# Streaming only the changed columns in the doubling inverse of a chunked delta-rule recurrence

## The reference

```python
def step(S, inp):
    r_t, w_t, k_t, v_t, kk_t, a_t = inp
    sa = jnp.einsum('bhvk,bhk->bhv', S, -kk_t)
    S = (S * w_t[:, :, None, :] + sa[..., None] * (kk_t * a_t)[:, :, None, :]
         + v_t[..., None] * k_t[:, :, None, :])
    return S, jnp.einsum('bhvk,bhk->bhv', S, r_t)
```

## Time and profile before

| What | Value |
|---|---|
| Time, median of 3 runs | 2047.01 us (2044.65 to 2049.49) |
| The profiled execution, its own time | 2045.39 us |
| Its span in the trace | 2043.6 us |
| TensorE busy | 1925.4 us, 94% |
| VectorE busy | 1462.8 us, 72% |
| ScalarE busy | 766.4 us, 38% |
| The recurrence stage in the trace | about 405 to 613 us |

### The profile page before, as it was taken

How to read it: one execution, slowest core, us unless ns; L and a number is a source line. 1 busy time by engine, 2 the same in 40 slices (tenths; PEclk the granted TensorE clock), 3 DMA queues, 4 the chain that set the end, 5 groups by cost and what they waited for, 6 DMA issues and landing times. The chain is left out here.

```text
span 2043.6 us, 35100 instructions
## 1 busy us (share of the span) xinstructions
PE 1925.4 (94%) x13881; PEld 1658.6 (81%) x13881; DVE 1462.8 (72%) x3152; ACT 766.4 (38%) x1177; POOL 333.4 (16%) x317
## 2 busy tenths in 40 slices
PE   6999998888989969999999999899779999999999
PEld 6998666677774469999999999799668888888887
DVE  4243343555545056999999999999968888888887
ACT  5332335222214133343334433477623333333332
POOL 1001100000000000333133222000322222322220
PEclk9999999999999979999999999899989999999999
DMA  3222111000003054886688668257979999999996
GB/s 132 86 92 83 32 32 62 25 30 3 3 3 165 0 187 128 327 309 243 240 320 320 251 240 306 66 173 215 299 266 366 334 341 338 341 345 339 339 336 253
DMA packets 175395, 407.24 MB, mean 199 GB/s; under 512 B 16768, under 2 KB 99968, under 8 KB 174208
## 3 DMA queue, kind: packets, MB, share of 16 engines
q1 hardware_dynamic: 132320, 255.96, 36.7%
q0 software_dynamic: 39744, 144.72, 18.8%
q10 hardware_dynamic: 3168, 4.33, 0.6%
HBM read 358.77 MB, written 46.14 MB: 198 GB/s over the span
## 5 line engine op out<-in xcount | busy, mean ns | idle before, releaser
L89 PE MATMUL eo_ps<-vh,e_wh 128*128 128x512 f32 x768 | 300.6, 391 | 12.6 <-DVE e_wl L1958 12.6
L90 PE MATMUL eo_ps<-vh,e_wl 128*128 128x512 f32 x768 | 300.2, 391 | 0.0
L91 PE MATMUL eo_ps<-vl,e_wh 128*128 128x512 f32 x768 | 300.2, 391 | 0.0
L1565 POOL DMA_INDIRECT g_stage<-in_u_rows,gidx x112 | 137.1, 1224 | 837.2 <-DVE gidx L1661 683.2
L1907 ACT CAST vh<-vraw 128x1024 fp32r<-128x1024 f32 x128 | 134.2, 1049 | 323.1 <-PE eo_ps L91 312.7
L1949 DVE TENSOR_TENSOR vl<-vraw,vh 128x1024 fp32r<-128x1024 f32 x128 | 156.7, 1224 | 73.2 <-ACT vh L1907 73.0
L1924 POOL DMA_INDIRECT e_rows<-in_v,gidx x128 | 137.2, 1072 | 391.2 <-DVE e_acc_t L1938 353.7
L89 PE MATMUL h_ps<-x2h,h_uh 128*128 128x384 f32 x520 | 180.9, 348 | 2.7 <-DVE h_ul L1418 2.7
L89 PEld LDWEIGHTS eo_ps<-vh,e_wh 128*128 128x128 f32 x768 | 145.1, 189 | 43.9 <-DVE vl L1949 10.0
L91 PE MATMUL h_ps<-x2l,h_uh 128*128 128x384 f32 x520 | 174.8, 336 | 0.0
L90 PE MATMUL h_ps<-x2h,h_ul 128*128 128x384 f32 x520 | 174.7, 336 | 0.0
(11 more groups left out here) (307 smaller groups left out, 4202.7 us busy)
## 6 DMA issues: line engine op xcount, KB each, us to landing
vraw<-in_v SPq DMA_DIRECT2D x128, 512.0 KB, 6.5
g_stage<-in_u SPq DMA_DIRECT2D x63, 512.0 KB, 6.6
e_hid<-HID_scratch SPq DMA_DIRECT2D x128, 192.0 KB, 6.9
h_uraw<-in_u SPq DMA_DIRECT2D x45, 512.0 KB, 5.2
wraw<-in_w_z SPq DMA_DIRECT2D x43, 512.0 KB, 3.5
HID_scratch<-h_hid SPq DMA_DIRECT2D x106, 192.0 KB, 4.1
G_scratch<-g_stage SPq DMA_DIRECT2D x16, 1024.0 KB, 11.8
gm<-G_scratch SPq DMA_DIRECT2D x128, 128.0 KB, 5.3
```

What stands on the lines that cost most here:

```text
L89: nc.tensor.matmul(out, a[0], b[0], start=start, stop=False)
L90: nc.tensor.matmul(out, a[1], b[0], start=False, stop=False)
L91: return nc.tensor.matmul(out, a[0], b[1], start=False, stop=stop)
L1565: nc.gpsimd.indirect_dma_start(urows[:, j % GBUF_R], None, d["u_rows"], bass.IndirectOffsetOnAxis(ap=gidx[:, j:j + 1], axis=0)).then_inc(r ...
```

## The change

Joining two blocks of size m changes only part of the columns: with kind 0 the first block's columns of each pair, with kind 1 the second's. The kernel before streams and adds all 48 columns, most of the results being zero. The changed kernel streams, writes, masks and adds only the columns of half `h` of each block pair. For levels 0, 1 and 2 (m = 2, 4, 8) these are 24 columns in runs of m. For levels 3 and 4 (m = 16, 32) the last pair is incomplete, and the columns are one run: 16 at level 3; at level 4 it is 32 for line 1079 and the mask, and 16 for line 1089 and the addition. In PSUM the results lie densely; in SBUF the moving operand of the matmuls and the operands of VectorE are read and written in these runs. The weights of every product stay 48 columns wide. Since `off` is also used as weights, the columns that aren't written must be zero, so `off` becomes one buffer per level and is cleared once at the start of the stage.

The widths of kind 0 and kind 1 differ at level 4 and their columns differ everywhere, so the one addition per group at line 998 becomes one per kind: four a level instead of two (at level 4 still two). Line 1079 of the next level waits only for the addition of kind 0 of its group.

```diff
-        off = sb("off", [P, NP4, C])
+        off = sb("off", [P, NLEV, NP4, C])
...
+        def width(lv, h):
+            m = LEVELS[lv]
+            return C // 2 if C % (2 * m) == 0 else min(m, C - h * m)
+
+        def blocks(x, lv, h):
+            m = LEVELS[lv]
+            if C % (2 * m) == 0:
+                return (x.rearrange("r (j h m) -> r j h m", h=2, m=m)[:, :, h] if len(x.shape) == 2 else
+                        x.rearrange("r q (j h m) -> r q j h m", h=2, m=m)[:, :, :, h])
+            c = slice(h * m, h * m + width(lv, h))
+            return x[:, c] if len(x.shape) == 2 else x[:, :, c]
...
+            nc.vector.memset(off[:], 0.0).then_inc(started, 1)
...
-                    nc.vector.tensor_tensor(off[0:R, g * HP:g * HP + HP],
-                                            ps[0:R, OFF[g], 0:HP * C].rearrange("p (a b) -> p a b", a=HP),
-                                            mlev[0:R, lv:lv + 1].broadcast_to([R, HP, C]), ALU.mult).then_inc(off_out, 1)
+                    nc.vector.tensor_tensor(
+                        blocks(off[0:R, lv, q], lv, 0),
+                        dense(ps[0:R, OFF[g], 0:HP * w].rearrange("p (a b) -> p a b", a=HP), lv, 0),
+                        blocks(mlev[0:R, lv:lv + 1].broadcast_to([R, HP, C]), lv, 0), ALU.mult).then_inc(off_out, 1)
...
-                    x0 = kinds(lv)[0]
-                    i = inv[0:R, b, x0:2, g * HP:g * HP + HP]
-                    nc.vector.tensor_tensor(i, i, ps[0:R, 4 + g, x0 * HP * C:2 * HP * C].rearrange(
-                        "p (x a b) -> p x a b", x=2 - x0, a=HP), ALU.add).then_inc(grown_out, 1)
+                    for x in kinds(lv):
+                        w = width(lv, x)
+                        i = blocks(inv[0:R, b, x, g * HP:g * HP + HP], lv, x)
+                        o = ps[0:R, 4 + g, x * HP * w:(x + 1) * HP * w].rearrange("p (a b) -> p a b", a=HP)
+                        nc.vector.tensor_tensor(i, i, dense(o, lv, x), ALU.add).then_inc(grown_out, 1)
...
-                        pe.wait_ge(grown_out, n * 2 + g - 1)
+                        pe.wait_ge(grown_out, grown_outs(c, lv - 1, g) + 1)
...
-                        mm = nc.tensor.matmul(ps[t, OFF[g], p % HP * C:p % HP * C + C], mb[t, b, p, 0:C],
-                                              inv[t, b, 0, p], start=True, stop=True)
+                        mm = nc.tensor.matmul(dense(ps[t, OFF[g], p % HP * w:p % HP * w + w], lv, 0), mb[t, b, p, 0:C],
+                                              blocks(inv[t, b, 0, p], lv, 0), start=True, stop=True)
...
-                            a, m = (inv[t, b, 1, p], off[t, p]) if x == 0 else (off[t, p], inv[t, b, 1, p])
-                            mm = nc.tensor.matmul(o, a, m, start=True, stop=True)
+                            a, m = (inv[t, b, 1, p], off[t, lv, p]) if x == 0 else (off[t, lv, p], inv[t, b, 1, p])
+                            mm = nc.tensor.matmul(o, a, blocks(m, lv, x), start=True, stop=True)
```

More of the change, by code:

```diff
@@ L889, in order, with dense, grown_outs @@
                 recur(NCH - 1, (NCH - 1) % 2, lv)
+        def width(lv, h):
[8 more added lines that the diff above has]
+            return x[:, c] if len(x.shape) == 2 else x[:, :, c]
+        def dense(x, lv, h):
+            m = LEVELS[lv]
+            if C % (2 * m) == 0:
+                return (x.rearrange("r (j m) -> r j m", m=m) if len(x.shape) == 2 else
+                        x.rearrange("r q (j m) -> r q j m", m=m))
+            return x
         def kinds(lv):
             return (0, 1) if lv < NLEV - 1 else (1,)
+        def grown_outs(c, lv, g=2):
+            return c * (4 * NLEV - 2) + sum(2 * len(kinds(i)) for i in range(lv)) + g * (len(kinds(lv)) if lv < NLEV else 0)
         def fox_piece(c, slot):
@@ L945, in _ @@
             nc.scalar.activation(last[:], L[:, :, bass.ds(C - 1, NCH, step=C)], ACT.Exp).then_inc(started, 1)
-            act.wait_ge(started, 4)
+            act.wait_ge(started, 5)
             scale(0, 0)
@@ L955, in _ @@
             nc.vector.memset(ex[:, :, 2, :, 0:1], 1.0).then_inc(started, 1)
+            nc.vector.memset(off[:], 0.0).then_inc(started, 1)
             dve.wait_ge(loaded, 48)
-            dve.wait_ge(started, 4)
+            dve.wait_ge(started, 5)
             def scale(c, b, part):
@@ L986, in level @@
                 n = c * NLEV + lv
+                w = width(lv, 0)
                 for g in range(2):
+                    q = slice(g * HP, g * HP + HP)
                     dve.wait_ge(offs, n * 2 + g + 1)
-                    nc.vector.tensor_tensor(off[0:R, g * HP:g * HP + HP],
-                                            ps[0:R, OFF[g], 0:HP * C].rearrange("p (a b) -> p a b", a=HP),
-                                            mlev[0:R, lv:lv + 1].broadcast_to([R, HP, C]), ALU.mult).then_inc(off_out, 1)
+                    nc.vector.tensor_tensor(
+                        blocks(off[0:R, lv, q], lv, 0),
+                        dense(ps[0:R, OFF[g], 0:HP * w].rearrange("p (a b) -> p a b", a=HP), lv, 0),
+                        blocks(mlev[0:R, lv:lv + 1].broadcast_to([R, HP, C]), lv, 0), ALU.mult).then_inc(off_out, 1)
                 if lv >= NLEV - 2 and c < NCH - 1:
@@ L1018, in _ @@
             pe.wait_ge(loaded, 48)
-            pe.wait_ge(started, 4)
+            pe.wait_ge(started, 5)
             def heads(pairs=range(NP4)):
@@ L1041, in prepare @@
                 if c >= 1:
-                    pe.wait_ge(grown_out, c * 2 * NLEV)
+                    pe.wait_ge(grown_out, grown_outs(c, 0, 0))
                     pe.wait_ge(tok_out, 6 * c)
@@ L1085, in level @@
                     for x in kinds(lv):
+                        w = width(lv, x)
                         for p, _, t in heads(range(g * HP, g * HP + HP)):
-                            o = ps[t, 4 + g, (x * HP + p % HP) * C:(x * HP + p % HP) * C + C]
-                            a, m = (inv[t, b, 1, p], off[t, p]) if x == 0 else (off[t, p], inv[t, b, 1, p])
-                            mm = nc.tensor.matmul(o, a, m, start=True, stop=True)
+                            o = dense(ps[t, 4 + g, (x * HP + p % HP) * w:(x * HP + p % HP) * w + w], lv, x)
+                            a, m = (inv[t, b, 1, p], off[t, lv, p]) if x == 0 else (off[t, lv, p], inv[t, b, 1, p])
+                            mm = nc.tensor.matmul(o, a, blocks(m, lv, x), start=True, stop=True)
                     mm.then_inc(grown, 1)
@@ L1105, in recur @@
                         pe.wait_ge(s_out, c)
-                    pe.wait_ge(grown_out, (c + 1) * 2 * NLEV)
+                    pe.wait_ge(grown_out, grown_outs(c + 1, 0, 0))
                     pe.wait_ge(tok_out, 6 * NCH if c == NCH - 1 else 6 * c + 12)
```

## The result

The changed kernel is slower: median 2082.4 us (2079.11 to 2090.22, four executions) against 2048.25 us (2044.65 to 2050.17, four). The ratio is 1.0174, with a 95% interval from 1.0142 to 1.0207, or 29 to 42 us. The sign is the one I forecast; the size is not. I had 7 us, and a range that ended at 2062.

A forecast was written before the change was run, and what follows sets the result against it. Bound by each level's chain of product, mask, product, addition, with the clock deciding: 2045.4 - 5.7 (path) + 0.9 (clearing) + 11.7 (clock) = 2052.3 us, 2053.9 against the median; 8-in-10 range 2040.5 to 2062.

The forecast's parts named there:

- The products don't come faster: Level matmuls stay 22 ns apart, set by the 48 weight columns; rival of 11 ns apart, 2021 us, chance 0.04.
- The shorter last record: Last matmul of a level's group: latency shorter by about 14 ns for 24 fewer columns, 18 for 32 fewer.
- The rule on a floor of some 25 ns for small matmuls: Skill's floor for matmuls of up to 64 columns: a level of 24 columns costs what one of 48 does.
- VectorE's operations: Level additions of 48 or 32 elements take 203 or 186 ns; masks 206, 222 or 189 in place of 256.
- Runs of two elements: VectorE's short-run operands: no row shows them; if they cost double, 48 elements take 253 ns and 1.5 us is lost.
- The clearing: Clearing `off`, 128 x 960 elements, on VectorE at the start: 0.9 us added, fully open before ScalarE's first exponential.
- The gain on the path: Shorter masks, additions and latencies over all levels and chunks of the recurrence stage: 5.7 us gained.
- The clock: TensorE's clock in the recurrence stage falls to 1.2 GHz more often as less is streamed: 11.7 us lost.
- The number of falls: Added clock falls, between none and about 18, taken as 9: behind levels 3 and 4, two in chunk 0.
- the price: Each clock fall costs 1.05 to 1.39 us in the preparation behind levels 3 and 4, taken as 1.3.
- The row that I took for a reason: Line 782, stage before: clock 0.50 under gapless matmuls on 32 rows, so rows streamed through seem to count.
- The rival by idle gaps: Skill's rule that idle gaps cause falls: none added, so no more falls; clock not minding, 2042.2 us, had 0.26.

The follow-up runs named there:

- narrow_rows64: The changed kernel with level products taking 64 rows of each head in place of 48, the added rows zero: 2047.12 us, ratio 0.9999.
- wide_rows64: wide_stream with 64 rows in place of 48 in the level products, the added ones zero: 2043.0 us, ratio 0.9967.
- wide_stream: The changed kernel with every level product streaming all 48 columns again, VectorE still working only on the changed columns: 2044.35 us, ratio 0.9977.
- narrow_012: The changed kernel with levels 3 and 4 streaming all 48 columns, only levels 0 to 2 narrow: 2057.07 us, ratio 1.0037.
- narrow_34: The changed kernel with levels 0 to 2 streaming all 48 columns, only levels 3 and 4 narrow: 2051.03 us, ratio 1.0020.
- narrow_stream_wide_vector: The changed kernel's narrow streams, but VectorE masks 96 and adds 192 elements as in the kernel before (inverse not right): 2101.36 us, ratio 1.0247.
- narrow_fill_32rows: The changed kernel plus unread matmuls where TensorE would wait, using 32 rows of the array: 2089.65 us, ratio 1.0188.

## Why the prediction was right in sign and wrong in size

**The products don't come faster: right.** 22 ns a record at 24 columns, as at 48; narrow_rows64 has 22 too, so 64 rows in place of 48 change nothing either. That it is the weights' 48 columns that set the distance is not shown: no run changed them, and a least distance of about 22 ns for any record this small would look the same. The shorter last record was worth less than I had: 199 ns for 24 columns and 191 to 195 for 16, at the high clock, against 208 for 48, so 9 and some 15 ns for my 14 and 18. The rule on a floor of some 25 ns for small matmuls (Trainium skill, TensorE: Matmul & The Clock Gate, "Back-to-back issue gap") gives the same answer to the question; the measured distance again lies a little under it.

**VectorE's operations: right.** 201 and 185 ns for 203 and 186, masks 208, 216 and 192 for 206, 222 and 189. Runs of two elements cost nothing that shows in these means.

**The clearing: right**, 0.86 us for 0.9, and 1.0 from the start of the clearing of PSUM to ScalarE's first exponential (4.84 us for 3.84).

**The gain on the path: 5.7 us forecast, 4.7 found.** Compare stages without falls: wide_rows64 has 194.5 us; the kernel before has 201.9, less two falls, 2 x 1.35 = 199.2. Those kernels stream 48 columns, so the shorter last record, which my sum counted at about 0.7 us over the chunks, is not in the 4.7.

**The clock.** The number of falls was near: 9 in the profiled stage, 7 more than before, where I had 9 more. That it came so near is luck, for their places are not mine. I had put them behind levels 3 and 4, and two more in chunk 0. Three of the nine begin behind level 3 or 4, in level 4 of chunk 6 and in the preparations of chunks 4 and 10. The other six begin in level 2, in chunks 2, 4, 5, 7, 8 and 10, and chunk 0 has none.

The step that failed is the price: "So a fall costs 1.05 to 1.39 us ... I take 1.3." I read that price from two falls of 3.5 us each and carried it over to a kernel whose falls last up to 27 us. A fall has no fixed price; in the changed kernel one cost 43.6 / 9 = 4.8 us. What has a nearly stable price is the time at 1.2 GHz. wide_rows64 has no fall in the stage; against its 194.5 us the changed kernel lost 238.1 - 194.5 = 43.6 us over 114.6, 0.38 us for each, and wide_stream 202.4 - 194.5 = 7.9 over 21.0, again 0.38. narrow_012, narrow_34 and narrow_rows64 give 0.37, 0.35 and 0.34. My own 1.39 us over 3.5 was 0.40, so the rate was in my rows; the length of the falls was not. The term is 0.38 x (114.6 - 7.0) = 41 us, not 11.7. With it the sum is 2045.4 - 4.7 + 0.9 + 41 = 2082.6, and the profiled execution took 2081.75. That is bookkeeping, not a forecast: the 114.6 us come from the trace that they explain.

In cause the term was right, and this is shown, not argued: give the columns back (wide_stream) and the loss is gone; keep the narrow streams alone (narrow_stream_wide_vector) and it is there; keep them and give them rows (narrow_rows64) and nearly all of it is gone.

**The row that I took for a reason was misread.** I argued from line 782, with 32 rows of the array, that a low clock under gapless matmuls comes from few rows. The trace of the kernel before shows that the clock had fallen earlier, while TensorE did nothing for 4.54 us:

```profile
355.96 1.25 PE L781 MATMUL lora_w_ps<-zT,g_up 128*128 128x264 f32 x2 [4.54 <-ACT r_L L742]
```

```profile
351.50:354.00 2.50, 0.00 (x0) 0.00 (x0) 0.00 (x0) 2.47 (x3) 0.00 (x0) 1.00 0.00 0
354.50:355.00 0.50, 0.00 (x0) 0.00 (x0) 0.50 (x1) 0.50 (x1) 0.00 (x0) 0.50 0.00 0
360.50:364.00 3.50, 3.50 (x9) 2.66 (x9) 1.82 (x2) 0.60 (x1) 0.00 (x0) 0.50 0.00 0
```

And it stayed low in the last of these stretches too, under matmuls of 128 rows and 512 columns. So that row says nothing of rows. That rows count is true here, but it is narrow_rows64 and narrow_fill_32rows that show it.

**The rival by idle gaps** (Trainium skill, TensorE: Matmul & The Clock Gate, "HAM oscillation — how this bites in real kernels") would have had no more falls and 2042.2 us. For a long gap the trace agrees with it: the fall at about 354.3 in the rows above. As the only cause the traces of the stage disagree with it. TensorE was idle for 15.1 of the 238.1 us in the changed kernel and for 19.7 of the 201.9 in the kernel before (by the busy times in their rows), and it is the changed kernel that fell nine times. wide_rows64 was idle for 16.4 us and didn't fall. The fall at about 454.5 came between products that follow one another, 0.7 us after a wait of 0.42 us, and the clock then read 0.50 through 5.00 of 5.00 us busy.

**What I should have seen.** I had bounded the number of falls, and only the number. The same rows ahead of the stage show a low clock that lasted 10 us, from 354.3 to 364.3, where the falls that I priced lasted 3.5. The upper bound of the range should have been the stage at 1.2 GHz nearly throughout, 0.38 to 0.40 us for each of its 200 us.

**Left open.** Why the falls last so unequally, from 3.5 to 27.3 us, in one kernel, and why most of them begin in level 2. How much the columns and how much the rows count. Each count of falls is from one execution; narrow_rows64's ten times spread the widest of all, so its 30 us at 1.2 GHz are one draw of many. Why narrow_stream_wide_vector lost 38 us more at 1.2 GHz than the changed kernel was not tried.

## What to carry to other kernels

Where streaming fewer columns brings the matmuls no closer together (here 22 ns at 24 and at 48), it saves nothing on TensorE and can cost the clock; narrow the vector work behind the product, and leave the product as wide as it comes for free. When a stage consists of small matmuls, look at the granted clock of its stretches and not at TensorE's busy share, and price a lower clock by time at 1.2 GHz: here 0.34 to 0.38 us lost for each us. Price the length of the falls too, not only their number. Rows and columns that cost no time are worth trying to fill, even with zeros.

## What the runs showed of the hardware that I had not expected

Rows of zeros help to hold the clock: 64 rows in place of 48 in 2464 of the stage's 4580 matmul records, with no other difference but GpSimd's clearing of the added rows at the start, brought the time at 1.2 GHz from 114.6 to 29.6 us in the profiled executions and the ratio from 1.0174 to 0.9999. The clock can stay at 1.2 GHz for 27.3 us, with TensorE busy for 19.90 of 22.00 us of it. Unread matmuls of 128 columns helped with 128 rows (65 us at 1.2 GHz) and not with 32 (117 us). And GpSimd cleared 128 x 960 elements in 0.90 us, about as fast as VectorE's 0.86.
